# GLA mixer of a two-layer decoder step: mixed values in pairs of array quarters, a moved projection tile, norms of the prompt rows ahead of the gate, and identity products in front

## The reference

```python
proj = h @ w_qkvr                      # q, k (384 each), v, r (768 each)
log_a = log_sigmoid((h @ a1) @ a2 + ab) / 16
# prompt: chunks of C = 64 rows, 4 heads, state S of 96 x 192 per head
inter = (q_c * exp(b)) @ S                       # b = cumsum(log_a) in the chunk
intra = causal(att) @ v_c
S = exp(b_end) * S + (k_c * exp(b_end - b)).T @ v_c
# sample: one row per sequence, with a state of its own that is read and returned
o = o * rsqrt(mean(o * o) + eps) * norm_g        # by head
out = o * silu(r)
```

## Time and profile before

| what | value |
|---|---|
| median of 3 runs | 1578.72 us (1574.31 to 1581.51) |
| the profiled execution's own time | 1572.76 us |
| its span, first to last instruction | 1570.5 us |
| mean granted TensorE clock | 0.895 |
| busy: PE, DVE, ACT | 78%, 26%, 15% |
| HBM read | 455.12 MB, 294 GB/s over the span |

### The profile page before, as it was taken

How to read it: one execution, slowest core, us unless ns; L and a number is a source line. 1 busy time by engine, 2 the same in 40 slices (tenths; PEclk the granted TensorE clock), 3 DMA queues, 4 the chain that set the end, 5 groups by cost and what they waited for, 6 DMA issues and landing times.

```text
span 1570.5 us, 20887 instructions
## 1 busy us (share of the span) xinstructions
PE 1226.8 (78%) x9280; PEld 663.1 (42%) x9280; DVE 405.3 (26%) x815; ACT 241.6 (15%) x634; POOL 18.5 (1%) x54
## 2 busy tenths in 40 slices
PE   6999979799676559675757999699866857956754
PEld 3678879685132115131314656277321313322311
DVE  4555674362110120110103433313101101101003
ACT  3223424221010001010002331122100100100100
POOL 2000000000000000000000000000000000000000
PEclk9989989999999987988988898599987986989987
DMA  9720201577999999999998421493999999999994
GB/s 308 223 81 28 46 7 59 203 270 303 409 409 409 409 408 407 409 409 409 409 375 283 126 57 34 141 373 125 409 409 410 409 409 407 409 409 409 409 409 182
DMA packets 147507, 463.64 MB, mean 295 GB/s; under 512 B 12891, under 2 KB 37245, under 8 KB 147213
## 3 DMA queue, kind: packets, MB, share of 16 engines
q1 hardware_dynamic: 145996, 457.78, 75.5%
q0 software_dynamic: 1408, 4.38, 0.9%
HBM read 455.12 MB, written 7.02 MB: 294 GB/s over the span
## 4 chain that ended last, share of the span: by engine, by line
PE 48%; DMA 42%; ACT 3%; SPq 3%; DVE 3%; issue 2%; POOL 0%; DVEq 0%; ACTq 0%; POOLq 0%
DMA slot<-in_exp_w_up 28%; DMA slot<-in_exp_w_down 8%; PE bank L1156 7%; PE bank L663 7%; DMA arena<-in_exp_w_up 5%; PE bank L1137 5%; PE bank L917 5%; PE bank L816 4%; PE bank L964 3%; PE bank L970 3%; PE bank L1167 3%; SPq L381 3%; DMA arena<-in_exp_w_down 2%; PE bank L790 1%; PE bank L914 1%
## 5 line engine op out<-in xcount | busy, mean ns | idle before, releaser
L1156 PE MATMUL bank<-slot,hT 128*32 128x512 f32 x1536 | 233.3, 726 | 138.5 <-DMA slot<-in_exp_w_up 138.4
L1156 PEld LDWEIGHTS bank<-slot,hT 128*32 128x32 f32 x1536 | 49.7, 123 | 306.1 <-DMA slot<-in_exp_w_up 179.2
L1755 DVE SCALAR_TENSOR_TENSOR mixedT<-mixedT,bank 128x512 f32<-128x512 f32 x16 | 11.0, 688 | 509.3 <-ACT mixedT L1312 509.3
L1156 PE MATMUL bank<-slot,mixedT 128*32 128x512 f32 x768 | 96.0, 641 | 38.4 <-DMA slot<-in_exp_w_down 31.4
L1156 PE MATMUL bank<-arena,hT 128*32 128x512 f32 x512 | 77.2, 682 | 37.3 <-DMA arena<-in_exp_w_up 37.3
L1167 PE MATMUL bank<-mixedT,arena 128*128 128x512 f32 (+1 forms) x192 | 92.6, 626 | 12.7 <-ACT mixedT L1321 12.7
L1312 ACT ACTIVATE mixedT<-bank 128x512 f32<-128x512 f32 x16 | 9.6, 597 | 537.3 <-PE bank L1156 537.3
L1137 PE MATMUL bank<-arena,h 128*128 128x128 f32 (+1 forms) x384 | 80.9, 348 | 12.0 <-DVE arena L1748 7.6
L1137 PEld LDWEIGHTS bank<-arena,h 128*128 128x128 f32 (+1 forms) x384 | 61.9, 220 | 36.3 <-issue 11.6
L1767 DVE TENSOR_TENSOR x<-bank,x 128x512 f32<-128x512 f32 (+1 forms) x96 | 66.0, 688 | 38.6 <-PE bank L1167 38.6
L816 PE MATMUL bank<-mixedT,slot 128*128 128x264 f32 x256 | 64.3, 408 | 9.7 <-issue 9.7
(11 more groups left out here) (470 smaller groups left out, 1437.7 us busy)
## 6 DMA issues: line engine op xcount, KB each, us to landing
slot<-in_exp_w_up SPq DMA_DIRECT2D x96, 2048.0 KB, 24.1
slot<-in_exp_w_down SPq DMA_DIRECT2D x48, 2048.0 KB, 23.9
arena<-in_exp_w_up SPq DMA_DIRECT2D x32, 2048.0 KB, 23.8
arena<-in_exp_w_down SPq DMA_DIRECT2D x16, 2048.0 KB, 23.7
slot<-in_w_in SPq DMA_DIRECT2D x6, 1536.0 KB, 7.7
slot<-in_w_out SPq DMA_DIRECT2D x4, 2048.0 KB, 8.9
slot<-in_w_in SPq DMA_DIRECT2D x3, 2048.0 KB, 7.8
slot<-in_w_in SPq DMA_DIRECT2D x5, 1024.0 KB, 7.2
```

The lines of the kernel that those rows point to most:

```text
L1156: last = pe.matmul(ps[bank + half][rows, :], lhs[:, rows], ring[buf][:, e, half * FF:(half + 1) * FF], start=first, stop=last_)
```

## The change

On PE: 30 identity products stand ahead of transpose_h(2). new_states(c0) issues two chunks' state products alternately (different row halves, different banks). mixed_values(u) issues for each head first both chunks' gatt products, then both chunks' state products. The sample update is split in halves of a row (two heads, one of the three banks 5 to 7); mixed_values(1) comes after half 5, the fourth r tile after half 9, the read-out last. On ACT the prompt rows' squares come before the fourth r tile is copied out, and gsq counts twice. On DVE a Newton round for the prompt's eight columns stands ahead of the gate's silu, the prompt's norms come after it, and the sample's four columns have a Newton round of their own. gs_add now counts halves.

```diff
+                for n in range(30):
+                    pe.matmul(ps[2 + n % 2][:, 0:128], ident[:, :], ident[:, :], start=True, stop=True)
                 transpose_h(2)
...
-                def new_state(c):
+                def new_states(c0):
-                    if c == 1:
+                    if c0 == 0:
                         pe.wait_ge(s["ga_out"], 1)
                         pe.wait_ge(s["sat_out"], 2)
-                    if c >= 2:
-                        pe.wait_ge(s["gz"], c - 1)
+                    else:
+                        pe.wait_ge(s["gz"], 2)
                     for i in range(4):
+                        for c in (c0, c0 + 1):
+                            rows = slice(C * (c % 2), C * (c % 2) + C)
...
-                def sample_kv(b):
+                def sample_kv(n):
+                    b, u = divmod(n, 2)
+                    if n >= 3:
+                        pe.wait_ge(s["gs_add"], n - 2)
                     else:
+                        pe.wait_ge(s["gz"], 4)
+                    for i in (2 * u, 2 * u + 1):
+                        last = pe.matmul(ps[5 + n % 3][0:96, 192 * (i % 2):192 * (i % 2 + 1)], gkm[0:TS, b, i, :], gv[0:TS, 2, 192 * i:192 * (i + 1)],
...
                 def mixed_values(u):
+                    pe.wait_ge(s["gz"], 2 * u + 1)
                     for i in range(4):
+                        o = lambda c: ps[O_BANK[u][i // 2]][C * (c % 2):C * (c % 2) + C, 192 * (i % 2):192 * (i % 2 + 1)]
                         for c in (2 * u, 2 * u + 1):
                             rows = slice(C * (c % 2), C * (c % 2) + C)
+                            last = pe.matmul(o(c), gatt[rows, u, i, :], gv[rows, u, 192 * i:192 * (i + 1)], start=True, stop=(c == 0))
+                        for c in (2 * u, 2 * u + 1):
                             if c > 0:
-                                pe.wait_ge(s["gz"], c)
+                                last = pe.matmul(o(c), gqh[0:96, i, C * c:C * (c + 1)], gZ[c][0:96, i, :], start=False, stop=True)
...
                 mixed_values(0)
-                for b in range(TS):
-                    sample_kv(b)
-                    if b == 3:
-                        tokens(w_in(6), 1)
-                pe.wait_ge(s["gs_add"], TS)
+                for n in range(6):
+                    sample_kv(n)
                 pe.wait_ge(s["p1_out"], 23)
                 mixed_values(1)
+                for n in range(6, 10):
+                    sample_kv(n)
+                tokens(w_in(6), 1)
+                for n in range(10, 2 * TS):
+                    sample_kv(n)
+                pe.wait_ge(s["gs_add"], 2 * TS)
...
-                for n in range(4):
+                for n in range(3):
                     out1(gr[:, n % 2, 384 * (n // 2):384 * (n // 2 + 1)], 128, 384)
+                for u in range(2):
+                    act.wait_ge(s["go_ps"], u + 1)
+                    for i in range(4):
+                        last = act.activation(junk((gl, ge)[u])[:, 192 * i:192 * (i + 1)], ps[O_BANK[u][i // 2]][:, 192 * (i % 2):192 * (i % 2 + 1)], ACT.Square, accum_out=g_ss(u, i, 128))
+                last.then_inc(s["gsq"], 1)
+                out1(gr[:, 1, 384:TOK], 128, 384)
...
+                dve.wait_ge(s["gsq"], 1)
+                scale(g_rs[:, 0:8], g_ssq[:, 0:8], width=192)
                 dve.wait_ge(s["g_tanh"], 1)
...
+                normed((0, 1))
+                dve.wait_ge(s["gsq"], 2)
+                scale(g_rs[:, 8:12], g_ssq[:, 8:12], width=192)
+                last = normed((2,))
                 mark(last, "t_dve", 11)
```

More of the change, by code:

```diff
@@ L595, in mixer1 @@
             def mixer1():
-                pool.wait_ge(s["gs_add"], TS)
+                pool.wait_ge(s["gs_add"], 2 * TS)
                 for n, a in enumerate((gS_early, gS_late)):
@@ L1058, in mixer1 @@
                 last.then_inc(s["ga_ps"], 1)
-                def new_state(c):
-                    rows = slice(C * (c % 2), C * (c % 2) + C)
-                    if c == 1:
+                def new_states(c0):
+                    if c0 == 0:
                         pe.wait_ge(s["ga_out"], 1)
                         pe.wait_ge(s["sat_out"], 2)
-                    if c >= 2:
-                        pe.wait_ge(s["gz"], c - 1)
+                    else:
+                        pe.wait_ge(s["gz"], 2)
                     for i in range(4):
-                        last = pe.matmul(ps[4 + 2 * (c % 2) + i // 2][0:96, 192 * (i % 2):192 * (i % 2 + 1)], khn[rows, c // 2, 96 * i:96 * (i + 1)],
-                                         gv[rows, c // 2, 192 * i:192 * (i + 1)], start=True, stop=True)
+                        for c in (c0, c0 + 1):
+                            rows = slice(C * (c % 2), C * (c % 2) + C)
+                            last = pe.matmul(ps[4 + 2 * (c % 2) + i // 2][0:96, 192 * (i % 2):192 * (i % 2 + 1)], khn[rows, c // 2, 96 * i:96 * (i + 1)],
+                                             gv[rows, c // 2, 192 * i:192 * (i + 1)], start=True, stop=True)
                     last.then_inc(s["gd_ps"], 1)
-                def sample_kv(b):
-                    if b >= 2:
-                        pe.wait_ge(s["gs_add"], b - 1)
-                    else:
-                        pe.wait_ge(s["gz"], b + 3)
-                    for i in range(4):
-                        last = pe.matmul(ps[4 + 2 * (b % 2) + i // 2][0:96, 192 * (i % 2):192 * (i % 2 + 1)], gkm[0:TS, b, i, :], gv[0:TS, 2, 192 * i:192 * (i + 1)],
+                def sample_kv(n):
+                    b, u = divmod(n, 2)
+                    if n >= 3:
+                        pe.wait_ge(s["gs_add"], n - 2)
+                    else:
+                        pe.wait_ge(s["gz"], 4)
+                    for i in (2 * u, 2 * u + 1):
+                        last = pe.matmul(ps[5 + n % 3][0:96, 192 * (i % 2):192 * (i % 2 + 1)], gkm[0:TS, b, i, :], gv[0:TS, 2, 192 * i:192 * (i + 1)],
                                          start=True, stop=True)
@@ L1098, in mixer1 @@
                 pe.wait_ge(s["kh_out"], 1)
-                new_state(0)
-                new_state(1)
+                new_states(0)
                 tokens(w_in(5), 1)
-                new_state(2)
-                new_state(3)
+                new_states(2)
                 tokens(w_in(6), 0)
@@ L2101, in mixer1 @@
                 dve.wait_ge(s["gla_in"], 32)
-                for b in range(TS):
-                    dve.wait_ge(s["gs_vps"], b + 1)
-                    for i in range(4):
+                for n in range(2 * TS):
+                    b, u = divmod(n, 2)
+                    dve.wait_ge(s["gs_vps"], n + 1)
+                    for i in (2 * u, 2 * u + 1):
                         last = dve.scalar_tensor_tensor(out=gS[b][0:96, i, :], in0=gS[b][0:96, i, :], scalar=gqh[0:96, i, TP + b:TP + b + 1],
-                                                        in1=ps[4 + 2 * (b % 2) + i // 2][0:96, 192 * (i % 2):192 * (i % 2 + 1)], op0=ALU.mult, op1=ALU.add)
+                                                        in1=ps[5 + n % 3][0:96, 192 * (i % 2):192 * (i % 2 + 1)], op0=ALU.mult, op1=ALU.add)
                     last.then_inc(s["gs_add"], 1)
+                dve.wait_ge(s["gsq"], 1)
+                scale(g_rs[:, 0:8], g_ssq[:, 0:8], width=192)
                 dve.wait_ge(s["g_tanh"], 1)
@@ L2116, in mixer1, with normed @@
                 O_BANK = [(2, 3), (0, 4)]
[L2117 to L2124, removed]
+                def normed(tiles):
+                    for t in tiles:
+                        m = TILES[t][1]
+                        for i in range(4):
+                            o = go[0:m, t, 192 * i:192 * (i + 1)]
+                            src = o if t == 2 else ps[O_BANK[t][i // 2]][:, 192 * (i % 2):192 * (i % 2 + 1)]
+                            last = dve.scalar_tensor_tensor(out=o, in0=src, scalar=g_rs[0:m, 4 * t + i:4 * t + i + 1], in1=gr[0:m, t, 192 * i:192 * (i + 1)],
+                                                            op0=ALU.mult, op1=ALU.mult)
+                    return last
+                normed((0, 1))
+                dve.wait_ge(s["gsq"], 2)
+                scale(g_rs[:, 8:12], g_ssq[:, 8:12], width=192)
+                last = normed((2,))
                 mark(last, "t_dve", 11)
```

13 lines of the change are left out of this document (3 added, 10 removed).

## The result

The changed kernel takes 1565.15 us (median of 6 runs, 1564.04 to 1567.09), the kernel before 1578.63 beside it (6 runs, 1574.31 to 1581.51). The ratio is 0.9933, with a 95% interval of 0.9913 to 0.9953: 10.6 us less, between 7.4 and 13.7. By the two medians it is 13.5 less. The forecast was 17.2 less, 1561.5 us, with a range of 1552 to 1571; the median lies inside that range and 3.7 us above the forecast.

The account below looks back on a forecast made before the run. The prediction took the second mixer's PE chain, ahead of the first expert, as the bound. Front -4.0, states -2.2 and tail -11.0 summed to -17.2 us, from a median of 1578.72 to 1561.5 us, range 1552 to 1571.

Parts of the forecast that it names:

- Front: Second mixer's start: identity products hold the clock; transposes -2.4, first feature -2.0, 0.4 us late: -4.0 us.
- the middle: Stretch from the end of the second 264-column feature to the first v tile; the forecast had no term for it.
- States: State products of two chunks issued in pairs overlap and take half the time, -1.1 for each of two calls: -2.2 us.
- Tail: From the end of the third r tile to t_dve 11: 47.5 us in the new order against 58.5, -11.0 us.
- updates 0 to 5: Tail, first six half-row sample updates after mixed_values(0): 4.2 us, at most 0.74 each.
- Updates 6 to 9: Tail, sample updates after mixed_values(1): 4.8 us taken at the low clock, 2.7 at full clock.
- the r tile: Tail, fourth r tile after the updates 6 to 9: 7.5 us, starting low; 5.4 at full clock.
- updates 10 to 15: Tail, last sample updates after the fourth r tile: 5.5 us with a fall of the clock on the way, else 4.8.
- DVE's chain: End of the tail: Newton, gate's silu, ACT's copies and sample squares, second Newton, sample norms without a gap: 15.1 us.
- the one where the pairs don't overlap: Rival: mixed_values(1) unpaired keeps its 13.3 us, gain only 10.5, 1568.2 us; 10% together with a low r tile.
- The rival with the clock high through the tail: Rival: the clock holds through the tail, 39.8 us there, -24.9 in all, 1553.8 us; chance 20%.
- The rival with low transposes: Rival: front transposes lose the clock, they and the first feature stay slow, -12.8 in all, 1565.9 us; chance 13%.

Follow-up runs that it names:

- e1: The kernel before with only the thirty identity products in front added: 1575.28 us beside 1575.31, ratio 0.9994.
- e2: The changed kernel without the thirty identity products in front: ratio 0.9947 to the kernel before.
- e11: The same program as e7, the changed kernel with sample updates and query spread 128 rows deep, run again: 1553.05 us, ratio 0.9851.
- e9: The changed kernel with sample updates and query spread 128 rows deep, without the thirty identity products in front: 1552.31 us, ratio 0.9834.
- e4: The changed kernel with the sample updates' products 128 rows deep instead of 8 (zero rows added): ratio 0.9870 to the kernel before.
- e7: The changed kernel with sample updates and the attention's query spread both 128 rows deep: 1548.13 us, ratio 0.9842.
- e8: e7 with fifty identity products added between the sample read-out and the tail's transposes: ratio 0.9813 to the kernel before.
- e10: The kernel before, in its old order, with only query spread and sample updates made 128 rows deep: 1563.62 us, ratio 0.9914.

## Why the prediction was right in direction and 4 to 7 us too far

The forecast is 3.7 us too far by the medians and 6.6 by the ratio. By its own steps, in the profile (forecast, measured):

- Front: -4.0, -3.3, and then +3.3 in the middle, which the sum put at no change without looking at it. **This is the step that failed**: the sum took the front's gain to arrive whole behind the middle. In its own stage the front did what was said. The products hide under DVE's norm, the clock held, and the transposes gave 2.0 of 2.4 (eight steps of 0.58 us, each with a copy by ACT of 0.48; the sum had 0.53 a step). But no timing shows the gain. Three pairs of kernels differ by the front alone: e1 and before, after and e2, e11 and e9. Their ratios differ by -0.0006, -0.0014 and +0.0017, on average nothing, where 3.3 us would be -0.0021; each difference is uncertain by some 0.002 to 0.004, so a worth of 2 us or so isn't excluded. Why the rest doesn't arrive is not settled. The middle took 50.6, 52.3 or 53.9 us without the front and 50.6 or 53.9 with it (8-row spread), so one profile each cannot say whether a clock held at the front is paid for there, or whether the middle varies by itself. Before's 50.6 is among the shortest and after's 53.9 the longest; if that is chance, the change is worth nearer 14 us by the profiles, about what the medians say. That front and middle are linked is not shown.
- States: -2.2, -1.5. Pairs overlap, as argued, but not wholly: a pair steps in 0.37 us (1.47 over 4), where a product alone took 0.28 (2.22 over 8); the forecast assumed half the time.
- Tail: -11.0, -9.25. The updates 0 to 5 took 5.9 and not 4.2, because the clock fell 2.1 us into them and not after 3.7 us or more; the forecast took the two earlier falls as its measure. Updates 6 to 9 took 5.4 (4.8 forecast), mixed_values(1) 6.70 (6.6), the r tile 7.64 (7.5), updates 10 to 15 5.0 (5.5), DVE's chain 14.89 (15.1). w_out did not hold anything up, though its second load took 20.4 us and not 10.5: issued at 991.5, landed at about 1012, and the output began at 1017.78.

The shortfalls are 4.0, 0.7 and 1.75: 6.45 us, and -17.2 becomes -10.75, the 10.6 of this pair of profiles but for rounding. The last two are terms that were mis-sized; the first is mostly a stage that the sum left out. That the range of 1552 to 1571 was wide enough to cover it is luck.

Of the rivals, the one where the pairs don't overlap is refuted: eight steps of 0.83 us, each with two quarters. The Trainium skill, "TensorEngine Tiling (Array Packing)", section "Restrictions and Gotchas", would have had the two row tiles that write to one bank take turns; the trace does not agree, the steps of e4 with two quarters are 0.47 us apart as those with one product are. The rival with the clock high through the tail did not happen here, but its sum for these stages (39.8 us) is nearly right: e4 took 39.1 for them, once the updates are 128 rows deep. The rival with low transposes happened in e11.

The version that beats both kernels keeps order and pairs and makes both 8-row products 128 rows deep: medians of 1546.84 to 1553.05 us for three kernels with and without fills (e7 and e11 are one, e8, e9), ratios 0.9813 to 0.9851, where after's interval begins at 0.9913. Their own intervals overlap, so these runs don't tell the fills' worth; the one without the front (e9) is the simplest.

## What to carry to other kernels

Where a stretch of PE work runs at a low granted clock, look at the products just ahead of the fall: in this tail they were products of 8 rows, with PE busy all through. Zero rows beneath the eight cost no time and kept the clock for the rest of the tail (30.7 us became 20.6). But look at each place by itself: in the middle the same edit shortened the low time, but in four profiles of five the clock had fallen ahead of the edited products. Two products side by side in the array cost no more time than one in mixed_values (0.47 us a step), and 0.37 against 0.28 us in the state products. A gain read in one stage of one profile is only a gain when the timed runs show it: the front's 3 us were there in seven profiles of eight, and no pair of timings could show them.

## What the runs showed that was not expected

- Depth of a product changed the clock and not the product's length at a given clock: eight update products took 2.84 us at the high clock with 8 rows (before, from 961.86) and with 128 (e10, from 964.64). Twelve of them took 5.97 us with 8 rows and a fall on the way, 4.14 with 128 at 1.00.
- The same program (e7, e11) held the clock through the front's transposes in one execution and lost it in another, 2.8 us apart in that stage.
- Pairs of 64-row products into different banks cost 0.37 us a step, pairs of 64-column products into one bank 0.47, no more than a single one.
